# First mixture of experts: six ring slots in two halves in place of three, with three later loads behind its chunks

## What is computed

```python
def moe_swiglu(u, w_router, wg, wu, wd):          # u: 256 tokens x 1024
    logits = (xf @ w_router).astype(F32)           # 8 experts
    vals, idx = lax.top_k(logits, TOP_K_EXPERTS)   # 2 of them for each token
    w = jax.nn.softmax(vals, axis=-1)
    gate = jnp.sum(jax.nn.one_hot(idx, N_EXPERTS, dtype=F32) * w[..., None], axis=1)
    for e in range(N_EXPERTS):
        y = y + gate[:, e:e + 1] * swiglu(xf, wg[e], wu[e], wd[e])
# swiglu(u, wg, wu, wd) = (silu(u @ wg) * (u @ wu)) @ wd, wg, wu: 1024 x 3584, wd: 3584 x 1024
```

## Time and profile before

| | us |
|---|---|
| runs, median (lowest to highest of 3) | 2227.4 (2223.37 to 2228.73) |
| profiled execution | 2224.47 |
| its span, first to last instruction | 2222.4 |
| TensorE busy in it | 2059.5 (93%) |
| mean granted TensorE clock | 0.966 |
| first mixture, first product to last | 752.7 to 1658.7 |

### The profile page before, as it was taken

How to read it: one execution, slowest core, us unless ns; L and a number is a source line. 1 busy time by engine, 2 the same in 40 slices (tenths; PEclk the granted TensorE clock), 3 DMA queues, 4 the chain that set the end, 5 groups by cost and what they waited for, 6 DMA issues and landing times.

```text
span 2222.4 us, 75430 instructions
## 1 busy us (share of the span) xinstructions
PE 2059.5 (93%) x34412; PEld 1795.4 (81%) x34412; DVE 596.2 (27%) x1360; ACT 406.1 (18%) x812; POOL 11.9 (1%) x20
## 2 busy tenths in 40 slices
PE   5977999999999999999999999999997987899998
PEld 3766888878647899999898989898986776787776
DVE  2577543341442201010101010101006252322222
ACT  2142000020453201111111111111113422211111
POOL 0000000000010000000000000000000000000000
PEclk8999999989889799999999999999999998899999
DMA  9725988643475499999999999999991200499996
GB/s 326 263 99 194 345 306 325 227 146 119 171 257 198 177 393 333 395 350 384 395 386 395 389 394 391 394 391 394 393 393 39 76 26 13 184 400 409 411 404 251
DMA packets 253306, 640.83 MB, mean 288 GB/s; under 512 B 15152, under 2 KB 21424, under 8 KB 247984
## 3 DMA queue, kind: packets, MB, share of 16 engines
q1 hardware_dynamic: 252384, 634.93, 76.0%
q10 hardware_dynamic: 848, 4.84, 0.6%
HBM read 638.68 MB, written 1.05 MB: 288 GB/s over the span
## 4 chain that ended last, share of the span: by engine, by line
PE 70%; DMA 20%; DVE 5%; ACT 2%; SPq 2%; issue 1%; DVEq 0%; POOLq 0%; POOL 0%; ACTq 0%
PE psum L757 23%; DMA ring<-in_moe_w_up 13%; PE psum L515 8%; DMA ring<-in_w_up 5%; PE psum L657 4%; PE psum L642 3%; PE psum L666 3%; PE psum L860 3%; PE psum L737 2%; SPq L2302 2%; PE psum L851 2%; PE psum L874 1%; PE psum L475 1%; PE psum L810 1%; PE psum L1256 1%; PE psum L1107 1%
## 5 line engine op out<-in xcount | busy, mean ns | idle before, releaser
L757 PE MATMUL psum<-uT,ring 128*64 128x80 f32 (+1 forms) x14336 | 563.6, 237 | 23.6 <-DMA ring<-in_moe_w_up 21.5
L757 PEld LDWEIGHTS psum<-uT,ring 128*64 128x64 f32 x14336 | 532.3, 137 | 53.0 <-DMA ring<-in_moe_w_up 37.0
L757 PE MATMUL psum<-arena,ring 128*64 128x80 f32 (+1 forms) x7168 | 269.7, 236 | 0.2 <-issue 0.2
L757 PEld LDWEIGHTS psum<-arena,ring 128*64 128x64 f32 x7168 | 264.1, 137 | 0.3 <-issue 0.3
L1780 DVE TENSOR_TENSOR arena<-arena,psum 128x288 f32<-128x288 f32 x56 | 25.5, 454 | 729.1 <-PE psum L757 729.1
L1407 ACT ACTIVATE arena<-psum 128x384 f32<-128x384 f32 x56 | 27.5, 492 | 696.6 <-PE psum L757 696.6
L1626 DVE SCALAR_TENSOR_TENSOR arena<-ring,cact,arena 128x512 f32<-128x512 f32 x168 | 126.2, 751 | 5.7
L515 PE MATMUL psum<-uT,ring 128*128 128x256 f32 (+1 forms) x496 | 114.1, 391 | 3.9 <-ACT uT L1312 3.6
L515 PEld LDWEIGHTS psum<-uT,ring 128*128 128x128 f32 (+1 forms) x496 | 95.7, 195 | 22.1 <-issue 7.8
L515 PE MATMUL psum<-arena,ring 128*128 128x256 f32 x384 | 86.2, 386 | 4.9 <-ACT arena L1312 3.6
L657 PE MATMUL psum<-uT,ring 128*128 128x256 f32 x352 | 79.7, 386 | 9.8 <-DMA ring<-in_ffn_w_gate 9.8
(11 more groups left out here) (420 smaller groups left out, 2048.6 us busy)
## 6 DMA issues: line engine op xcount, KB each, us to landing
ring<-in_moe_w_gate SPq DMA_DIRECT2D x224, 512.0 KB, 11.0
ring<-in_moe_w_up SPq DMA_DIRECT2D x224, 512.0 KB, 9.8
ring<-in_moe_w_down SPq DMA_DIRECT2D x224, 512.0 KB, 11.1
ring<-in_w_ada SPq DMA_DIRECT2D x36, 2048.0 KB, 14.2
ring<-in_w_up SPq DMA_DIRECT2D x19, 2048.0 KB, 11.2
ring<-in_w_down SPq DMA_DIRECT2D x19, 2048.0 KB, 9.8
ring<-in_w_gate SPq DMA_DIRECT2D x19, 2048.0 KB, 10.5
ring<-in_ffn_w_gate SPq DMA_DIRECT2D x5, 2048.0 KB, 7.9
```

Source lines behind the costliest of these rows:

```text
L757: mm = pe.matmul(out(HD * hc), w[:, c0 + HD * hc:c0 + HD * hc + HD], x, skip_group_check=True, **kw)
```

## The change

The first mixture gets a second set of three slots, `M.slots_odd`. Even chunks of a tile (0, 2, 4, 6) live in the first half of the ring, odd ones (1, 3, 5) in the second, and there are 24 landing semaphores in place of 12. SP loads chunks 0 and 1 at the start, and then a granule of chunk `c + 2` when the same granule of chunk `c` has been used. The three loads `ctx2`, `win2.0`, `win2.1` no longer stand between the first chunks and the loop but behind all chunks of the mixture, in the same slots as before. On TensorE the products of a chunk become a function `chunk_products`; since the slots alternate and a tile has seven chunks, the inner loop now does two chunks in each of three passes, and the seventh chunk is written out behind it. Products, their order and their number are the same.

```diff
-        mix = [Mix("m1", E1, F1, 96, 12, posi[:, 0:64], 80), Mix("m2", E2, F2, 64, 3, posi[:, 64:128], 0)]
+        mix = [Mix("m1", E1, F1, 96, 24, posi[:, 0:64], 80), Mix("m2", E2, F2, 64, 3, posi[:, 64:128], 0)]
...
+        mix[0].slots_odd = [(SLOT1 + 3 + j) % NSLOT for j in range(3)]
...
+                def chunk_products(n, slots, land, nth, W):
+
+                    wg, wu = (slot_view(slots[r], KT, 512) for r in range(2))
+                    wd = slot_view(slots[2], 4, D)
+                    for k in range(KT):
+                        if k % 2 == 0:
+                            pe.wait_ge(land[k // 2], nth * 16 + 16)
+                        for f in range(4):
+                            mm = block(lambda r: psum[r:r + HD, 0, N * f:N * f + W], wg[:, k, :], M.xg[:, k, 0:W], P * f,
+                                       start=(k == 0 and f == 0), stop=(k == KT - 1))
+                        if k % 2:
+                            mm.then_inc(M.g, 1)
+                    for k in range(KT):
+                        if k % 2 == 0:
+                            pe.wait_ge(land[4 + k // 2], nth * 16 + 16)
+                        for f in range(3):
+                            mm = block(lambda r: psum[r:r + HD, 1, N * f:N * f + W], wu[:, k, :], M.xg[:, k, 0:W], P * f,
+                                       start=(k == 0 and f == 0), stop=(k == KT - 1))
+                    mm.then_inc(M.ua, 1)
+                    pe.wait_ge(M.sg, n + 1)
+                    for k in range(KT):
+                        mm = block(lambda r: psum[r:r + HD, 0, 4 * N:4 * N + W], wu[:, k, :], M.xg[:, k, 0:W], P * 3,
+                                   start=(k == 0), stop=(k == KT - 1))
+                        if k % 2:
+                            mm.then_inc(M.u, 1)
+                    for f in range(4):
+                        if f in (0, 3):
+                            pe.wait_ge(M.hid, n * 2 + (1 if f == 0 else 2))
+                        pe.wait_ge(land[8 + f], nth * 16 + 16)
+                        for k in range(KT):
+                            mm = block(lambda r: psum[r:r + HD, 2 + k // 4, N * (k % 4):N * (k % 4) + W], wd[:, f, :],
+                                       M.hidden[:, 0, N * f:N * f + W], P * k, start=False, stop=False)
+                        mm.then_inc(M.dn, 1)
+
...
-                    with pe.Fori(0, CH) as c:
-                        n = q * CH + c
...
+                    with pe.Fori(0, CH // 2) as p:
+                        chunk_products(q * CH + 2 * p, M.slots, M.land[0:12], q * (CH - CH // 2) + p, W)
+                        chunk_products(q * CH + 2 * p + 1, M.slots_odd, M.land[12:24], q * (CH // 2) + p, W)
+                    chunk_products(q * CH + CH - 1, M.slots, M.land[0:12], q * (CH - CH // 2) + CH // 2, W)
...
+                slot = (M.slots_odd if c % 2 else M.slots)[r]
...
-                sp.dma_start(dst, w.rearrange("e (k p) n -> p (e k) n", p=P)).then_inc(M.land[i], 16)
+                    dst = slot_view(slot, 4, D)[:, j:j + 1, :]
...
-            for i in range(12):
-                if i % 4 == 0:
-                    sp.wait_ge(*freed[occupant[M.slots[i // 4]]])
-                granule(0, 0, i)
-            for n in names[BEFORE_MOE1:AFTER_MOE1]:
-                load(n)
+            for c, slots in enumerate((M.slots, M.slots_odd)):
+                for i in range(12):
+                    if i % 4 == 0:
+                        sp.wait_ge(*freed[occupant[slots[i // 4]]])
+                    granule(0, c, i)
             sp.wait_ge(s_tab, 1)
             last = sp.value_load(M.tab[0:1, TABLE:TABLE + 1], min_val=0, max_val=TABLE - 2)
             with sp.Fori(0, last) as q:
                 e = sp.value_load(M.tab[0:1, bass.ds(q, 1)], min_val=0, max_val=E1 - 1)
-                for c in range(CH - 1):
+                for c in range(2, CH):
                     for i in range(12):
-                        sp.wait_ge(*granule_used(q, c, i))
-                        granule(e, c + 1, i)
-                e = sp.value_load(M.tab[0:1, bass.ds(q + 1, 1)], min_val=0, max_val=E1 - 1)
+                        sp.wait_ge(*granule_used(q, c - 2, i))
+                        granule(e, c, i)
+                for c in (1, 0):
+                    e = sp.value_load(M.tab[0:1, bass.ds(q + 1, 1)], min_val=0, max_val=E1 - 1)
+                    for i in range(12):
+                        sp.wait_ge(*granule_used(q, CH - 1 - c, i))
+                        granule(e, c, i)
+            e = sp.value_load(M.tab[0:1, bass.ds(last, 1)], min_val=0, max_val=E1 - 1)
+            for c in range(2, CH):
                 for i in range(12):
-                    sp.wait_ge(*granule_used(q, CH - 1, i))
-                    granule(e, 0, i)
-            e = sp.value_load(M.tab[0:1, bass.ds(last, 1)], min_val=0, max_val=E1 - 1)
-            for c in range(CH - 1):
-                for i in range(12):
-                    sp.wait_ge(*granule_used(last, c, i))
-                    granule(e, c + 1, i)
-            for r in range(3):
-                occupant[M.slots[r]] = f"first{r}"
-                freed[f"first{r}"] = granule_used(last, CH - 1, 4 * r + 3)
-            for n in names[AFTER_MOE1:]:
+                    sp.wait_ge(*granule_used(last, c - 2, i))
+                    granule(e, c, i)
+            for c, slots in ((CH - 2, M.slots_odd), (CH - 1, M.slots)):
+                for r in range(3):
+                    occupant[slots[r]] = f"first{c}.{r}"
+                    freed[f"first{c}.{r}"] = granule_used(last, c, 4 * r + 3)
+            for n in names[BEFORE_MOE1:]:
                 load(n)
```

More of the change, by code:

```diff
@@ L744, in first_mixture @@
                 N, CH = M.N, M.CH
-                wg, wu = (slot_view(M.slots[r], KT, 512) for r in range(2))
-                wd = slot_view(M.slots[2], 4, D)
                 def clear_y():
@@ L2297, in granule @@
                     w = w[:, 2 * P * j:2 * P * j + 2 * P, 512 * c:512 * c + 512]
-                    dst = slot_view(M.slots[r], KT, 512)[:, 2 * j:2 * j + 2, :]
+                    dst = slot_view(slot, KT, 512)[:, 2 * j:2 * j + 2, :]
                 else:
                     w = w[:, 512 * c + P * j:512 * c + P * j + P, :]
-                    dst = slot_view(M.slots[r], 4, D)[:, j:j + 1, :]
-                sp.dma_start(dst, w.rearrange("e (k p) n -> p (e k) n", p=P)).then_inc(M.land[i], 16)
+                    dst = slot_view(slot, 4, D)[:, j:j + 1, :]
+                sp.dma_start(dst, w.rearrange("e (k p) n -> p (e k) n", p=P)).then_inc(M.land[12 * (c % 2) + i], 16)
             def granule_used(q, c, i):
```

## The result

The changed kernel is slower. Its median is 2260.6 us (2259.3 to 2263.3, five runs) against 2227.4 of before; the ratio is 1.0151, with a 95% interval of 1.0137 to 1.0164. The forecast was 2215, the range ended at 2246. The profiled execution took 2262.9 us.

The account below looks back on a forecast made before the run. The first mixture was taken as bound by TensorE until 993.7 us and by transfers after that. A 17 us gain from the ring less 5 us of instruction fetch gave -12: 2227.4 to 2215 us, whole range 2207 to 2246.

Parts of the forecast that it names:

- What bounds the kernel: First mixture: bound by TensorE until 993.7 us (wide tiles), by the transfers after that (narrow tiles, 16.06 us per chunk).
- The second half of the ring: Six slots in the first mixture: 40 chunks to load from 993.7 us, not 41; gain 17 us, upper bound 20.0.
- The moved loads: Context rows and two projection tiles, loaded behind the mixture's chunks, land before they are wanted; cost nothing, nearest margin 14 us.
- SP's work: One more table value loaded per tile of the mixture, covered by work already in the queue; cost nothing.
- the odd chunk's early load: Before the mixture, in place of context rows and projection tiles: 1.05 MB extra, 3 us, hidden; cost nothing.
- The growth of TensorE's program: Mixture tile grows from 3.75 to 9.8 instruction blocks; inner loop kept, outer jump not; 5 us on the path.
- 5 us in the wide tiles: One paid outer jump, tile 0 to 1, with transfers nearly idle: 5 us on the path, bounds 0 and 9.2.
- 25 us in the narrow tiles, hidden under 645: Five outer jumps in the narrow tiles: 607 plus 25 is 632 us, under the 645 of the transfers.
- B: Inner loop also falls out of TensorE's instruction store, every jump paid: +19 us, 2246, far end 2271; chance 0.22.
- A: TensorE's instruction store holds a tile, or the fetch hides under the scatter: no code cost, 2210; chance 0.22.
- C: Ring gain doesn't appear: queue limits transfers, or stock is used up before 993.7; 0 +- 3, 2227; chance 0.14.

Follow-up runs that it names:

- aligned kernel: Changed kernel with seventh chunk not written out, odd chunk branched over in the last pass, and never-executed instructions (92 and 44) ahead of the tile loops: 2213.6 us.
- shifted kernel: Changed kernel with 68 and 36 never-executed instructions ahead of the two tile loops, so the inner loop touches 8 blocks and not 7: 2306.4 us.
- three-slot kernel with 6.8 blocks: Kernel before (three slots, its loads) with TensorE's inner loop running one chunk in six passes and the seventh chunk written out: 2255.8 us.
- shifted twin: The three-slot kernel with 6.8 blocks plus 92 and 44 never-executed instructions ahead of the two tile loops, so a tile touches 7 blocks: 2229.5 us.
- six-slot ones: Changed kernel with odd chunk branched over in a fourth pass, seventh not written out: 2237.8 us; the same with never-executed instructions ahead of the loops: 2213.6 us.

## Why the prediction was wrong, step by step

**What bounds the kernel** was read rightly. Half the bytes take the narrow tiles to 102.6 us, where the prediction had 7 x 13.33 + 9.4 = 102.7.

**The second half of the ring** was sized rightly: 17 us forecast, 16.9 in the trace of the aligned kernel, 16 and 18 between medians of pairs with equally small code, kept in the one and fetched again in the other. The moved loads, SP's work and the odd chunk's early load cost nothing, as costed.

**The growth of TensorE's program** is the step that failed. Its frame held. The jump to the start of a tile misses the store, at 3.0 us in the narrow tiles where 5 was taken. The inner loop stays (in the narrow tile above, its second and third pass have no stop), and some ten blocks per tile were forecast where 11 are fetched. What it left out is the price of the blocks in sequence. The prediction counted stalls at jumps only, and read from one stall of 0.19 us at 1005.1 that a block is usable 4.6 us after it is asked for, near enough to the 4.5 us of a block of products to be called hidden. That row was in the first narrow chunk, where the DMA share was only 0.80 after the gap between tiles, as the window of the kernel before shows:

```profile
995.00:1005.00 10.00, 9.93 (x288) 9.82 (x285) 0.71 (x2) 1.77 (x2) 0.00 (x0) 1.00 0.80 260
```

In the steady narrow tiles the interval was 5.6 to 6.2 us, and eleven blocks per tile, not one jump, have to be paid for. So the term "5 us in the wide tiles" measured 8.9. It was taken there because the transfers at a wide transition were called nearly idle, and that is a misreading: the earlier trace rows have them at a share of 0.76. The term "25 us in the narrow tiles, hidden under 645" measured 80: from 1002.4 to 1689.0 it is 686.6 us where the sum had 607. That is 13 us per tile, and against the 645 of the transfers TensorE is the bound. The whole gain of the stock was spent before it could show.

**The rivals.** B had the right sign and the right condition (program fetch makes TensorE the bound in the narrow tiles), and the measured 2261 lies between its 2246 and its far end of 2271. That is luck: it named the wrong mechanism, misses of the inner loop, and so its chance was taken from whether that loop stays. It stays, and the loss came all the same. In the narrow tiles B has 17 jumps at 3.5 us, 10 us a tile, and the trace has 13, for fetches that B left out. The shifted kernel shows B's own mechanism in part, in the third pass of the wide tiles, at 2306. A fell: the store doesn't hold a tile of 9.8 blocks. C fell: with the code kept the ring delivers its 16 us.

**The Trainium skill.** "Runtime: NRT & Kernel Launch", section "Instruction fetch mechanics", has 2048 instructions for TensorE. The runs agree: 7 blocks touched and one ahead are kept (60 blocks in all, none from 1110 to 1640), 8 and one ahead are not (87 and 114). Its branch rule with a window of two pages doesn't hold here: loops over 6.8 blocks ran without a fetch. The same section calls the cost of a block boundary mostly hidden. At a DMA share of 0.67 the runs agree (83 blocks more for 7 us, 2177.5 against 2170.3); at 1.02 the boundaries shown in the first pass cost 0.2 to 2.2 us each.

## What to carry to other kernels

When an edit writes a loop body out more often, count the instructions of everything up to the outermost jump back, and where they lie in the blocks: up to 7 blocks touched cost nothing here, an eighth cost 24 to 26 us. Instruction fetches are transfers too (q8 stands among the queues of the 16 DMA engines), so code that streams was nearly free at a DMA share of 0.67 and dear in the stage that is bound by the transfers. A stock of one more chunk is worth 16 to 18 us here and still lost 33 together with the longer program, so test a buffering change with the program's size held fixed before judging it.

## What was not expected of the hardware

- Some 100 never-executed instructions ahead of a loop changed the time by 24 and 26 us one way and by 46 us the other, with the same work executed.
- A tile that touches one block too many doesn't fetch one block again but nine at a time: the three-slot kernel with 6.8 blocks has 87, its shifted twin 60, the six-slot ones 114 and 60. Nine at three of six jumps cost 26 us with three slots, nine at all six 24 us with six.
- Stalls of TensorE cost more where the stock is small: the long program cost 59 us with three slots (2287.4 against 2228.1) and 47 with six (2260.6 against 2213.6 for the kernel whose code is kept).
- In or behind a stop of 3.0 us, and of 7.0 us, the granted clock fell to 1.2 GHz, for some 3 and 10 us, so part of a stop was paid a second time in slower products.
